# Forgetting attention: the exponential ahead of the high copy, reciprocal and division in one step, and the output's split inside the last maps

## The reference

```python
def forgetting_attention(q, k, v, log_f):
    scale = dh ** -0.5
    cum = jnp.transpose(jnp.cumsum(log_f, axis=1), (0, 2, 1))

    def block(i):
        ...
        s = jnp.einsum('bqhd,bshd->bhqs', qb, k, preferred_element_type=jnp.float32) * scale
        s = s + (cq[..., :, None] - cum[..., None, :])
        p = masked_softmax(s, kpos[None, :] <= tpos[:, None])
        return jnp.einsum('bhqs,bshd->bqhd', p.astype(v.dtype), v)

def odd_mixer(h, w_in, b_f, w_out):
    q, k, v, f = split_cols(h @ w_in, ODD_SPLITS)
    log_f = jax.nn.log_sigmoid((f + b_f).astype(jnp.float32))
    o = forgetting_attention(q, k, v, log_f)   # q, k, v by head
    return o.reshape(bsz, seq, FOX_W) @ w_out
```

## Time and profile before

| what | value |
|---|---|
| runs | 2468.31, 2468.32, 2468.55 us, median 2468.32 |
| profiled execution | 2466.31 us, its span 2464.5 us |
| busy share of the span | PE 96%, PEld 78%, DVE 58%, ACT 43%, POOL 14% |
| the stage of the maps | 794.0 to 1018.8 us of the span |

### The profile page before, as it was taken

One profiled execution on the slowest core, in us unless ns is written; L12 is line 12 of the kernel. 1 busy time (PEld: TensorE's weight loads), 2 busy tenths in 40 slices (PEclk: granted clock), 3 DMA queues, 4 the chain that ended last, 5 costly groups with the idle time before them and its releaser, 6 DMA issues.

```text
span 2464.5 us, 31535 instructions
## 1 busy us (share of the span) xinstructions
PE 2373.0 (96%) x11862; PEld 1915.7 (78%) x11862; DVE 1430.6 (58%) x2350; ACT 1048.0 (43%) x1788; POOL 343.0 (14%) x324
## 2 busy tenths in 40 slices
PE   8999899999999999799999999899999999999998
PEld 7877788888887777688888867677888777678887
DVE  3545655655655676456556559847533568666333
ACT  3756654322334565443223334454422344445223
POOL 0000111000000332200000136301100233111001
PEclk9999999999999999899999999999999999999999
DMA  5211003443332111134334322111223222102321
GB/s 200 91 52 44 2 27 101 148 152 120 130 128 94 52 58 55 34 111 145 138 120 153 112 69 69 62 34 32 97 94 103 77 69 69 43 27 69 111 94 52
DMA packets 58036, 211.73 MB, mean 86 GB/s; under 512 B 6432, under 2 KB 6560, under 8 KB 57888
## 3 DMA queue, kind: packets, MB, share of 16 engines
q1 hardware_dynamic: 57456, 208.86, 24.7%
q10 hardware_dynamic: 432, 0.85, 0.1%
HBM read 207.60 MB, written 2.10 MB: 85 GB/s over the span
## 4 chain that ended last, share of the span: by engine, by line
PE 82%; DVE 7%; issue 5%; ACT 4%; POOL 2%; DMA 0%; SPq 0%; ACTq 0%; DVEq 0%; POOLq 0%
PE bank L462 75%; PE last_bank L462 4%; PE bank L472 3%; DVE arena L1163 1%; POOL hv L2113 1%; DVE arena L2392 1%; DVE arena L2394 1%; ACT wparts L573 1%; POOL rstd L632 0%; ACT arena L826 0%; DVE small L838 0%; DVE arena L1019 0%; DMA ring<-weights_dram 0%; DVE small L2086 0%; DVE arena L2727 0%
## 5 line engine op out<-in xcount | busy, mean ns | idle before, releaser
L462 PE MATMUL bank<-hT,wparts 128*128 128x512 f32 x5520 | 1329.8, 397 | 5.5 <-DMA cb_sb<-cb_dram 4.3
L462 PEld LDWEIGHTS bank<-hT,wparts 128*128 128x128 f32 x5520 | 1035.0, 190 | 237.7 <-issue 23.1
L577 DVE TENSOR_TENSOR wparts<-ring,wparts 128x1024 fp32r<-128x1024 f32 x290 | 367.3, 1267 | 419.7 <-ACT wparts L573 419.4
L462 PE MATMUL bank<-arena_r,wparts 128*128 128x512 f32 x2400 | 552.4, 391 | 2.2 <-DVE arena_r L607 2.2
L462 PEld LDWEIGHTS bank<-arena_r,wparts 128*128 128x128 f32 x2400 | 450.9, 188 | 96.5 <-DVE arena_r L607 3.2
L573 ACT ACTIVATE wparts<-ring 128x1024 fp32r<-128x1024 f32 x332 | 348.1, 1049 | 159.6 <-PE bank L462 127.6
L577 POOL TENSOR_TENSOR wparts<-ring,wparts 128x1024 fp32r<-128x1024 f32 x42 | 101.1, 2408 | 213.0 <-ACT wparts L573 212.9
L603 ACT ACTIVATE arena_r<-arena 128x512 fp32r<-128x512 f32 x76 | 47.2, 629 | 177.9 <-POOL arena L2951 91.7
L462 PE MATMUL last_bank<-arena 128*128 128x64 f32 x780 | 107.0, 273 | 8.0 <-DVE arena L861 4.4
L462 PEld LDWEIGHTS last_bank<-arena 128*128 128x128 f32 x780 | 99.3, 194 | 16.7 <-issue 11.5
L472 PE MATMUL bank<-cf_sb,arena 128*128 128x128 f32 (+4 forms) x624 | 99.7, 280 | 11.6 <-DMA cf_sb<-cf_dram 5.0
(11 more groups left out here) (294 smaller groups left out, 2360.8 us busy)
## 6 DMA issues: line engine op xcount, KB each, us to landing
ring<-weights_dram SPq DMA_DIRECT2D x388, 512.0 KB, 3.3
arena<-x_dram SPq DMA_DIRECT2D x4, 512.0 KB, 5.9
out_dram<-arena SPq DMA_DIRECT2D x4, 512.0 KB, 4.0
rot<-rot_dram SPq DMA_DIRECT2D x1, 512.0 KB, 10.7
rot<-rot_dram ACTq DMA_DIRECT2D x1, 512.0 KB, 3.2
cf_sb<-cf_dram SPq DMA_DIRECT2D x1, 416.0 KB, 9.0
cb_sb<-cb_dram SPq DMA_DIRECT2D x1, 264.0 KB, 9.9
vecs<-vec_dram ACTq DMA_DIRECT2D x1, 258.5 KB, 5.9
```

The costliest lines, as they stand in the source:

```text
L462: i = pe.matmul(*args, **kw)
L577: eng.tensor_tensor(wparts[:, slot, 1, :, :], ring[:, p % RAW, :, :], wparts[:, slot, 0, :, :].bitcast(F32), ALU.subtract)\
```

## The change

Four edits are made in the functions of the maps.

1. In `act_fox` the exponential of map i-1 is issued ahead of the high copy of map i-3, not behind it.
2. In `dve_fox` the reciprocal of map i-1 is issued in step i behind the low part of map i-3. Before, that of map i-2 stood ahead of it. `pool_fox` divides map i-1 in step i, before it was map i-2.
3. The addition of the two halves of a head moves one step later on DVE (i % 4 is 1), and there is one step more.
4. `act_o1` and `dve_o1` are gone. The blocks of `o1` are split at steps 55 (blocks 0 and 1), 56 (2 and 3), 57, 58 and 62 (4, 5 and 6) and behind the last step (7). The low parts are written over `o1` itself (`Pair`), and the high ones wait for what was last read in their place. The list `order` gives the steps behind the projections one 1 each, 14 in all.

```diff
+        o1_at = A.at
         o1 = A.take(KD, SEQ)
...
-        oT1 = Area().take_r(2, KD, SEQ)
+        oT1 = Pair(Area().take_r(KD, SEQ), Area(o1_at).take_r(KD, SEQ))
...
+        def hi_of_output(act, k):
+            act.wait_ge(*dve_made["fox", "out", 2 * k + 1])
+            if k < 4:
+                act.wait_ge(*dve_made["q1", KD - 1, 1, "lo", 0])
+                act.wait_ge(*dve_made["k1", KD - 1, 1, "lo", 1])
+            else:
+                act.wait_ge(*filled["fox", "s", {4: 51, 5: 55, 6: 59, 7: 63}[k]])
+            act_hi(act, oT1[:, 0, k, :], o1[:, k, :], ("ot1", k))
+
+        def lo_of_output(dve, k):
+            dve_lo(dve, oT1[:, 0, k, :], oT1[:, 1, k, :], o1[:, k, :], ("ot1", k))
+
         def act_fox(act):
-            for i in range(M1 + 5):
-                if 3 <= i < M1 + 3:
-                    j = i - 3
-                    h, qt = divmod(j, NT)
-                    act.wait_ge(*filled["fox", "t", j])
-                    if qt == 0 and h >= 2:
-                        act.wait_ge(*filled["fox", "o", h - 2])
-                    act.activation(fox_turned(j, 0), turned_map(j), ACT.Copy).then_inc(*act_made.mark(("fox", "hi", j)))
+            for i in range(M1 + 6):
                 if 1 <= i < M1 + 1:
                     j = i - 1
                     W = maps[j]["width"]
@@ -2065,6 +2071,13 @@
                     act.activation(Pb1[:, j % 3, 0:W], banks["fox", "s", j][:, 0:W], ACT.Exp, bias=mx1(j),
                                    accum_out=sm1(j)).then_inc(*act_made.mark(("fox", "p", j)))
                     banks.drain(("fox", "s", j), "act_made")
+                if 3 <= i < M1 + 3:
+                    j = i - 3
+                    h, qt = divmod(j, NT)
+                    act.wait_ge(*filled["fox", "t", j])
+                    if qt == 0 and h >= 2:
+                        act.wait_ge(*filled["fox", "o", h - 2])
+                    act.activation(fox_turned(j, 0), turned_map(j), ACT.Copy).then_inc(*act_made.mark(("fox", "hi", j)))
                 if i >= 8 and i % NT == 0:
                     h = (i - 8) // NT
                     side = h % 2
@@ -2073,10 +2086,13 @@
                         act.wait_ge(*dve_made["fox", "out", h - 2])
                     act.activation(swap1[HALF[side], :], banks["fox", "o", h][HALF[1 - side], :], ACT.Copy)\
                        .then_inc(*act_made.mark(("fox", "swap", h)))
-                yield
+                for k in SPLIT_AT.get(i, ()):
+                    hi_of_output(act, k)
+                yield
+            hi_of_output(act, KD - 1)
...
 
         def dve_fox(dve):
-            for i in range(M1 + 5):
+            for i in range(M1 + 6):
                 if 1 <= i < M1 + 1:
                     j = i - 1
                     W = maps[j]["width"]
@@ -2085,49 +2101,43 @@
                         dve.wait_ge(*act_made["fox", "p", j - 3])
                     dve.tensor_reduce(mx1(j), banks["fox", "s", j][:, 0:W], AX.X, ALU.max, negate=True)\
                        .then_inc(*dve_made.mark(("fox", "max", j)))
-                if 2 <= i < M1 + 2:
-                    j = i - 2
-                    dve.wait_ge(*act_made["fox", "p", j])
-                    dve.reciprocal(sm1(j), sm1(j)).then_inc(*dve_made.mark(("fox", "inv", j)))
                 if 3 <= i < M1 + 3:
                     j = i - 3
                     dve.wait_ge(*act_made["fox", "hi", j])
                     dve.tensor_tensor(fox_turned(j, 1), turned_map(j), fox_turned(j, 0).bitcast(F32), ALU.subtract)\
                        .then_inc(*dve_made.mark(("fox", "lo", j)))
                     banks.drain(("fox", "t", j), "dve_made")
-                if i >= 8 and i % NT == 0:
-                    h = (i - 8) // NT
+                if 1 <= i < M1 + 1:
+                    j = i - 1
+                    dve.wait_ge(*act_made["fox", "p", j])
+                    dve.reciprocal(sm1(j), sm1(j)).then_inc(*dve_made.mark(("fox", "inv", j)))
+                if i >= 9 and i % NT == 1:
+                    h = (i - 9) // NT
                     c, side = divmod(h, 2)
                     dve.wait_ge(*act_made["fox", "swap", h])
                     dve.tensor_tensor(o1[HALF[side], c, :], banks["fox", "o", h][HALF[side], :], swap1[HALF[side], :],
                                       ALU.add).then_inc(*dve_made.mark(("fox", "out", h)))
                     banks.drain(("fox", "o", h), "dve_made")
-                yield
+                for k in SPLIT_AT.get(i, ()):
+                    lo_of_output(dve, k)
+                yield
+            lo_of_output(dve, KD - 1)
...
         def pool_fox(pool):
-            for i in range(M1 + 5):
-                if 2 <= i < M1 + 2:
-                    j = i - 2
+            for i in range(M1 + 6):
+                if 1 <= i < M1 + 1:
+                    j = i - 1
                     p = Pb1[:, j % 3, 0:maps[j]["width"]]
                     pool.wait_ge(*dve_made["fox", "inv", j])
                     pool.tensor_scalar(p, p, sm1(j), None, ALU.mult).then_inc(*pool_made.mark(("fox", "scaled", j)))
                 yield
 
-        order = [0, 0, 0] + spread(6, 8) + spread(9, 8) * (KD - 2) + [0] + [1] * (M1 + 5)
+        SPLIT_AT = {55: (0, 1), 56: (2, 3), 57: (4,), 58: (5,), 62: (6,)}
+        order = [0, 0, 0] + spread(6, 8) + spread(9, 8) * (KD - 2) + [0]
+        order += [1] * (M1 + 6 - 56)
         then(alternate(order, project(items[4:], None, None, vt1, vt_free=filled["v1", "nat", 0], pool=POOLS[0], norm=h1),
                        (act_fox, pe_fox, dve_fox, pool_fox)))
 
-        def act_o1(act):
-            act.wait_ge(*filled["fox", "s", M1 - 1])
-            for k in range(KD):
-                act.wait_ge(*dve_made["fox", "out", 2 * k + 1])
-                act_hi(act, oT1[:, 0, k, :], o1[:, k, :], ("ot1", k))
-
-        def dve_o1(dve):
-            for k in range(KD):
-                dve_lo(dve, oT1[:, 0, k, :], oT1[:, 1, k, :], o1[:, k, :], ("ot1", k))
-
-        then(act=act_o1, dve=dve_o1)
```

## The result

| kernel | median, us | runs, us | ratio to before, 95% interval | profiled span, us |
|---|---|---|---|---|
| before | 2468.44 | 2468.31 to 2471.18 (4) | 1 | 2464.5 |
| after | 2483.66 | 2481.40 to 2485.05 (4) | 1.0058 [1.0041, 1.0076] | 2479.6 |

One more execution of before ran beside after, hence four. The change costs 15.2 us by the medians and 15.1 us by the two profiled spans. I had forecast 7.2 more. The sign and the place were right, the size was half of what came. All but 0.3 us of it lies in the attention stage. Behind the start of the output product (the 1018.8 of before) before runs 1445.7 us to its end and after 1445.9.

A forecast was written before the change was run, and what follows sets the result against it. PE was taken to bound the weave at 27.53 us a pair, the DVE-ACT loop after the change; 7.1 + 1.2 - 2.2 - 1.3 + 2.4 = +7.2 us on the median 2468.32 gave 2475.5 us, range 2464 to 2484.

The forecast's parts named there:

- rival C: Weave: PE's bound and the DVE-ACT loop delay each other at times, 7.3 us more, 2483 us; chance 0.15.
- six pairs of heads: 1st to 13th output product: the DVE-ACT loop takes 172.3 us, 28.7 a pair, against 165.2; +7.1 us.
- first pair: 794.0 to 814.5 us: same loop with six projection steps for eight, a sixth of the cost; +1.2 us.
- tail: Map 54 to the last head's product: shorter loop spent on seven L607, plus 1 us for the clock; +2.4 us.
- end: wait for L607: Behind the last head's product: PE's wait for the output split goes, as most parts are ready; -2.2 us.
- clock of the output product, and all behind its start: Start of the output product: PE runs on without the gap, losing less at half clock; -1.3 us.
- every step goes DVE, ACT, DVE with nothing side by side: Changed weave: max, exp, sum read, hi, lo, inv and next max follow in line; 28.7 us a pair.
- only every second step had to go around this loop: Weave before the change: hi ran beside max and exp beside lo, the loop hidden under PE's 27.53 us a pair.
- whether POOL ran or not: DVE's L577 took 1224 to 1227 ns in all 19 cases, so contention with POOL's division was given nothing.
- Rival D: Weave: POOL's division holds up DVE's L577 by up to its full length, 22 us more, 2497 us; chance 0.03.
- A: Whole stage: the loop doesn't bind and PE's waits for POOL go, -15.3 us, 2453 us; chance 0.10.
- B: Weave: the loop just fits at 27.5 us a pair without the 7.5 us waits, -1.1, 2467 us; chance 0.22.

The follow-up runs named there:

- e2: Before with the reciprocal and division a step earlier and the halves' addition a step later, exponential order and split unchanged: 2453.19 us, ratio 0.9944.
- e3: After with the high copy put back ahead of the exponential, all else kept: 2453.71 us, ratio 0.9945 to before.
- e6: After plus an extra DVE reduction, read by nobody, ahead of each max: 2504.02 us, ratio 1.0144 to before.
- e7: After plus the same extra DVE reduction behind each max: 2480.67 us, ratio 1.0052 to before.
- e8: e3 plus an extra DVE reduction, read by nobody, ahead of each max: 2470.78 us, ratio 1.0012 to before.
- e5: After with POOL dividing only 16 columns of each map, the rest left undivided: 2475.12 us, ratio 1.0028 to before.
- e4: After with the whole output split behind the last map again: 2481.69 us, ratio 1.0055 to before.
- e9: Before with only the output split moved into steps 55 to 62 and behind the last: 2467.28 us, ratio 0.9995.
- e1: Before with only the exponential issued ahead of the high copy: 2476.53 us, ratio 1.0038.
- run 156: Not a label of a run: the words say that PE works 156 us without one gap in the six pairs of e3.

## Why the prediction was half right

The measured 2483.66 us lies within 0.4 us of the upper end of my range, 2464 to 2484. That end was set by rival C, whose cause the runs don't bear out, so it was luck that the range held. What was right is the mechanism in the weave and the wait at the end; the two large terms, for the six pairs and for the tail, were too small.

| term | predicted, us | measured, us |
|---|---|---|
| six pairs of heads | +7.1 | +9.5 |
| first pair | +1.2 | +1.8 |
| tail | +2.4 | +5.9 |
| end: wait for L607 | -2.2 | -2.4 |
| clock of the output product, and all behind its start | -1.3 | +0.1 |
| sum on the span | +7.2 | +15.1 (0.2 more from the stage's later start) |

**The mechanism held.** The step "every step goes DVE, ACT, DVE with nothing side by side" is what the trace of after shows, e2 and e3 show that edit 1 alone makes it, and e6 with e7, and the waits of DVE and ACT, that it sets the pace. The waits that were to go went, and those that were to come came. Where I said that before "only every second step had to go around this loop" I had the old loop too short: e8 and e3 put it between 25.1 and 26.3 us a pair. The forecast didn't use it.

**The six pairs: the argument on contention failed.** Without contention my 28.7 us a pair was near: the pairs of e5 behind the first took 28.84. What the sum left out is the 0.69 us a pair for which L577 and L591 are held up, all of it in line on DVE; in the means of after it is 18 L577 at 78 ns more and 33 L591 at 79, 4.0 us in the six pairs. I had written that L577 took 1224 to 1227 ns "whether POOL ran or not". The rows gave the durations, and not what POOL did at the time; the order of time shows that it ran beside one L577 in three, for 0.25 us, and never beside L591. Edit 2 moved the division from beside lo, with its input in PSUM, to beside whatever follows the reciprocal, and that is L577 or L591 four times a pair. Rival D named the mechanism, at a price far too high (22 us), and the forecast had no term for a small one. For the rest my sum of 172.3 us was 1.6 too long (174.7 less 4.0 is 170.7), so the two errors partly cancelled. The reason is the first pair, 2.4 us shorter than the others in after (27.08 against 29.5), where I had divided the whole evenly by six; six times 28.84 would be 173.0.

**The tail: the split was mis-sized.** My +2.4 is -2.8 for the loop without the splits (1.0 for the clock in it) and +5.2 for seven L607 and their waits. Measured, the loop without them gave -1.4 (e4, 32.9 against 34.2) and the splits cost +7.3 (after against e4). With the high copy first the same splits cost 3.3 (e3 against e2) and 4.2 (e9 against before), less than my 5.2; behind edit 1 they cost more. From one exponential to the next, after against e4, the 7.3 lie as follows: 1.8 from map 54 to 55 and 1.9 from 55 to 56, where two L607 each stand in the queue; 1.8 over the three steps with one L607 each; 0.5 from 58 to 59 and 1.2 from 62 to 63. The first of them in after:

```profile
996.09 1.60 DVE L607 TENSOR_TENSOR arena_r<-arena,arena_r 128x512 fp32r<-128x512 f32 x2 [0.16 <-ACT arena_r L603]
997.61 0.68 DVE L1019 SCALAR_TENSOR_TENSOR arena<-bank,rstd 128x512 f32<-128x512 f32 x1
998.34 0.42 PEld L472 LDWEIGHTS bank<-cf_sb,arena 128*128 128x128 f32 x4 [3.94 <-DVE arena L1019]
998.34 0.66 PE L472 MATMUL bank<-cf_sb,arena 128*128 128x128 f32 x4 [3.52 <-DVE arena L1019]
```

The two L607 take 1.60, where I had 0.61 each; a division of 384 columns that starts at 996.02 runs beside them and takes 1.78 for its 1.24. L1019, the last values, is queued behind them, and PE waits 3.5 us for it, in e4 1.8. The 0.5 and the 1.2 us (from 62 to 63 it is 3.79 us in after and 2.56 in e4) have no L607 in them. There DVE's max waits for PE's scores, 3.4 us in the tail of after and 1.7 in that of e4, and the difference of 1.7 is the two steps together. The granted clock differs as well. PE is granted 0.57 from 1018 to 1031 in after, where it is busy 7.5 of 13 us:

```profile
1018.00:1031.00 13.00, 7.46 (x29) 5.33 (x26) 5.65 (x14) 5.14 (x13) 4.36 (x4) 0.57 0.00 0
```

Over the whole tail it is 0.69 in after against 0.83 in e4. I had put 1 us on the clock, from 0 to 3. So about 1.7 of the 7.3 come by way of PE's own slower work; how much of the other 5.6 is clock and how much queueing no run separates, and e4's is one execution, its fastest.

**The end was right, its clock term not.** PE goes on from the last head's product without waiting:

```profile
1031.33 2.61 PE L462 MATMUL last_bank<-arena_r 128*128 128x512 f32 x8 [1.41 <-DVE arena_r L2107]
1033.74 2.87 PE L462 MATMUL bank<-arena_r,wparts 128*128 128x512 f32 x6
```

The wait for L607 of 2.2 us is gone. The clock over the next 10 us is 0.84 against 0.80, which is 0.4 us of work at full clock and not 1.3, and behind the start of the output product the kernel is no shorter at all.

**The rivals.** A, at 2453 us, is what e2 and e3 did, with the loop's old order: the room was there, and edit 1 spent it. B rested on my softest term, the waits on ACT's halves, put at 7.5 us. In the rows of after they are 4.5, 1.7 and 1.3 before L1049, L577 and L591, 7.5 again. C gave nearly the measured time, 2483, by a cause that the runs don't bear out: in the six pairs of after DVE and ACT never wait for PE, so PE's bound delays the loop nowhere, and without contention the pairs take 28.84 (e5), where my loop alone has 28.7.

**Singles don't add up.** Edit 1 alone is +9.4 us by its ratio, edits 2 and 3 alone -13.8, edit 4 alone -1.2, together -5.6, and the whole change is +14.3. The gain of the early reciprocal is time in which PE no longer waits. Once the loop sets the pace there is none to gain, and the edit costs: 28.48 us a pair in e1, where the reciprocal still stands ahead of lo and so in DVE's wait for hi, 28.84 in e5 and 29.52 in after. Of that 1.04 us, 0.68 is contention. The other 0.36 came with edits 2 and 3; that it is the reciprocal's new place in line fits the trace, but no run shows it by itself.

## What to carry to other kernels

Before two instructions change places in an engine's queue, write down the cycle that the queues then make: from one instruction on the first engine through the second and back to the next of its kind, with everything queued between them. If neither engine waits for a third one, that cycle sets the pace, and the third one's waits cost nothing (e1). Its length against the bound of now is the forecast, and shares of busy time don't show it: here DVE at 67% and ACT at 53% set the pace. To find out on a chip which piece of a queue is in the cycle, put the same dead work ahead of a suspected instruction and behind it. And a duration read from the trace of before holds for what ran beside it there, so when the change moves an engine's work to another time, look up what it will stand beside.

## What I had not expected of the hardware

A division on POOL and a two-input operation on DVE, both in SBUF, slow each other, but not by any fixed share of the time that they overlap. L577 at 937.49, which overlaps with a division for 0.75 us, took its usual 1.23. L577 at 947.67, with 0.84, took 1.46. In the first the division had begun 0.49 us earlier, in the second 0.08. In the six pairs the division of 384 columns was never longer than alone (1.24), and that of 256 columns went from 0.93 to 1.28 when it began inside a run of L591. In the tail of after, beside L607, a division of 384 columns took 1.78 and one of 128 columns, at 1006.33, 1.49 for 0.60. That is 0.89 more, where the L607 beside it takes 0.69 in all. I can't say what decides which of the two is held up. With one DVE input in PSUM no slowdown is seen: L1049, beside a division in after and not in before, takes 692 ns in both.

A loop through DVE and ACT, with PE in part of it, that is at most 1.2 us a pair shorter than PE's 26.27 (estimated in e8) lets PE run 156 us without one gap (e3). I had thought that two bounds so close would disturb each other.
